# Depthwise taps in four column groups on TensorE, and products over 768 tokens in two halves of 384 columns

## What is computed

```python
def conv_module(h, w_pw1, w_dw, b_dw, ln_g, ln_b, w_pw2):
    u = h @ w_pw1
    a, gate = jnp.split(u, 2, axis=-1)
    u = a * jax.nn.sigmoid(gate)
    u = lax.conv_general_dilated(
        u, w_dw[:, None, :].astype(u.dtype), window_strides=(1,),
        padding=[(CONV_PAD, CONV_PAD)], dimension_numbers=('NWC', 'WIO', 'NWC'),
        feature_group_count=D_MODEL) + b_dw
    u = jax.nn.silu(layer_norm(u, ln_g, ln_b))
    return u @ w_pw2
...
        mod_l = jnp.split(sc @ w_mod[i] + b_mod[i], 6, axis=-1)
        hl = modulate(rms_norm(xl, norm1_g[i]), mod_l[0], mod_l[1])
        hc = modulate(rms_norm(xc, norm1_g[i]), mod_c[0], mod_c[1])
        if m == 0:
            ol = conv_module(hl, *cargs)
            oc = conv_module(hc, *cargs) if with_ctx else None
```

## Time and profile before

| what | value |
|---|---|
| median of 3 runs (range) | 2349.9 us (2349.07 to 2354.52) |
| the profiled execution | 2348.4 us |
| its span, mean granted clock of PE | 2346.1 us, 0.974 |
| PE, weight load, DVE, ACT, POOL busy | 95%, 76%, 60%, 34%, 28% of the span |
| products at L609 in the chain that ended last | 48% of the span |
| taps in that chain | 2% (PE, L2470) and 1% (DVE, L1748) |

### The profile page before, as it was taken

How to read it: one execution, slowest core, us unless ns; L and a number is a source line. 1 busy time by engine, 2 the same in 40 slices (tenths; PEclk the granted TensorE clock), 3 DMA queues, 4 the chain that set the end, 5 groups by cost and what they waited for, 6 DMA issues and landing times.

```text
span 2346.1 us, 30707 instructions
## 1 busy us (share of the span) xinstructions
PE 2223.6 (95%) x11666; PEld 1787.7 (76%) x11666; DVE 1417.1 (60%) x1872; ACT 807.3 (34%) x1145; POOL 667.5 (28%) x377
## 2 busy tenths in 40 slices
PE   6999969899999999998999999999997999899997
PEld 5677748788888888885457888887886888788885
DVE  5789982654444445544563754655418552699997
ACT  3212134211111111333663311111322543677775
POOL 0000014233333333431444344444542234011001
PEclk8999979999999999999999999999999999899999
DMA  9455532432222222220002233333232234599996
GB/s 309 156 160 169 198 124 81 179 138 63 63 63 63 63 63 63 66 72 10 10 1 64 83 98 92 97 98 113 72 90 63 63 76 153 188 394 403 406 405 252
DMA packets 248208, 312.12 MB, mean 133 GB/s; under 512 B 13642, under 2 KB 199595, under 8 KB 235827
## 3 DMA queue, kind: packets, MB, share of 16 engines
q1 hardware_dynamic: 236764, 275.33, 34.8%
q0 software_dynamic: 6688, 25.69, 2.8%
q10 hardware_dynamic: 4663, 9.79, 1.1%
HBM read 286.13 MB, written 24.65 MB: 132 GB/s over the span
## 4 chain that ended last, share of the span: by engine, by line
PE 84%; DVE 10%; ACT 2%; POOL 1%; DMA 1%; issue 1%; DVEq 0%; POOLq 0%; SPq 0%; ACTq 0%
PE acc L609 48%; PE acc L3013 8%; PE pb L3031 4%; PE acc L2524 3%; PE acc L2735 2%; PE pa L2749 2%; PE pb L2470 2%; PE pb L2762 2%; PE acc L661 2%; PE acc L643 2%; PE acc L2588 1%; DVE csum L1748 1%; DVE hid_hi L1813 1%; PE acc L690 1%; PE pa L2410 1%
## 5 line engine op out<-in xcount | busy, mean ns | idle before, releaser
L548 POOL TENSOR_TENSOR wlo<-raw,whi 128x1024 fp32r<-128x1024 f32 x180 | 449.5, 2498 | 907.1 <-ACT whi L537 887.0
L537 ACT ACTIVATE whi<-raw 128x1024 fp32r<-128x1024 f32 x188 | 198.4, 1059 | 890.3 <-PE acc L609 836.1
L609 PE MATMUL acc<-ah,whi 128*128 128x256 f32 (+1 forms) x1256 | 393.7, 362 | 5.0 <-DVE sg L2008 2.6
L609 PE MATMUL acc<-al,whi 128*128 128x256 f32 (+1 forms) x1256 | 389.4, 359 | 0.0
L609 PE MATMUL acc<-ah,wlo 128*128 128x256 f32 (+1 forms) x1256 | 388.9, 358 | 0.0
L609 PEld LDWEIGHTS acc<-ah,whi 128*128 128x128 f32 x1256 | 235.6, 189 | 48.3 <-issue 8.9
L609 PEld LDWEIGHTS acc<-ah,wlo 128*128 128x128 f32 x1256 | 236.7, 188 | 36.8
L609 PEld LDWEIGHTS acc<-al,whi 128*128 128x128 f32 x1256 | 236.7, 188 | 36.1 <-issue 0.5
L1833 DVE SCALAR_TENSOR_TENSOR x<-acc,mod,x 128x512 f32<-128x512 f32 (+1 forms) x174 | 109.7, 658 | 232.2 <-PE acc L609 232.1
L1037 DVE TENSOR_TENSOR expert_lo<-expert_pair,expert_hi 128x1024 fp32r<-128x1024 f32 x192 | 224.5, 1219 | 14.5 <-ACT expert_hi L1032 14.5
L1032 ACT ACTIVATE expert_hi<-expert_pair 128x1024 fp32r<-128x1024 f32 x192 | 201.4, 1059 | 63.4 <-PE acc L3013 40.1
(11 more groups left out here) (501 smaller groups left out, 3684.4 us busy)
## 6 DMA issues: line engine op xcount, KB each, us to landing
raw<-in_w_ff SPq DMA_DIRECT2D x128, 512.0 KB, 4.0
mod_raw<-in_w_mod SPq DMA_DIRECT2D x80, 512.0 KB, 5.8
expert_pair<-in_expert_w_gate SPq DMA_DIRECT2D x32, 1024.0 KB, 8.0
expert_pair<-in_expert_w_up SPq DMA_DIRECT2D x32, 1024.0 KB, 7.7
expert_pair<-in_expert_w_down SPq DMA_DIRECT2D x32, 1024.0 KB, 7.3
raw<-in_w_in SPq DMA_DIRECT2D x30, 512.0 KB, 3.8
raw<-in_conv_w_pw SPq DMA_DIRECT2D x24, 512.0 KB, 8.8
expert_rows_dram<-zero_rows POOLq DMA_DIRECT2D x1, 12288.0 KB, 38.1
```

Source lines behind the costliest of these rows:

```text
L537: e.eng.activation(whi[e.n["q"] % 2][:, :], raw[r][:, :], ACT.Copy).then_inc(S["hi_ready"], 1)
L548: e.eng.tensor_tensor(wlo[b][:, :], raw[e.n["g"] % RING][:, :], whi[b][:, :].bitcast(F32), ALU.subtract).then_inc(S["lo_ready"], 1)
L609: ins = e.eng.matmul(o, w, m, start=keys.index(key) == n, stop=len(keys) - 1 - keys[::-1].index(key) == n)
```

## The change

**Products.** `HALVES` takes the place of `FULL` wherever a product runs over 768 tokens: two matmuls of 384 columns in place of 256 and 512. The output then lies in columns 128 to 896 of the bank, so that each half is in a PSUM bank of its own; those who read it look there (`unit_at`, `all_cols`).

**Taps.** `TAP_BLOCKS` blocks of four taps in place of single taps on PE: 12 taps of tiles 0 to 5, 16 of tile 6 and 24 of tile 7. For each group `g` of 32 channels, `shifted[32 s + c, g, :]` holds `upb` of channel 32 g + c shifted by s, for the four shifts s; one matmul of 128 rows by 32 columns then adds four taps of 32 channels, and four of them, one for each group, write four different column groups of PE's array. So a block of four taps costs eight matmuls, and reads `shifted` with an offset of four per block. ACT issues 16 DMAs per tile that fill `shifted` (`shift_rows_of`, between `take_taps(i + 1)` and the copy of the second chunk), each 32 rows of 791 to 803 f32, about 101 KB. The matrices `tap_rows` are made by POOL, one tensor_tensor of 128 x 128 per block (`place_taps`), from 14 further columns of constants; the identity matrices scaled by ACT go. There is one buffer `shifted`: its fill waits for PE's taps of the tile before. PE does the taps of tile i - 1 where those of tile i stood; DVE takes the sum in an addition of its own (L1787) after tap 14.

**Others.** Both `split_low` of a tile go from DVE to POOL. `gated` stands after tap 10. Six more DMAs of constants.

```diff
-PE_TAPS = (0, 6, 6, 6, 6, 6, 6, 9)
+TAP_BLOCKS = (3, 3, 3, 3, 3, 3, 4, 6)
+GATE_AT = (16, 10, 10, 10, 10, 10, 10)
+SUMS_AT = (18, 15, 15, 15, 15, 15, 13, 6)
...
+    HALVES = [(0, TOK // 2, 1), (TOK // 2, TOK, 0)]
...
-        def make_diagonals(i):
-
-            act.wait_ge(S["taps_ready"], i + 1)
-            if i >= 2:
-                act.wait_ge(S["conv_summed"], i - 1)
-            for j in range(PE_TAPS[i]):
-                t = TAPS - PE_TAPS[i] + j
-                ins = act.activation(diag[:, j, :], mats[:, M_ID, :], ACT.Copy, scale=taps[i % 2][:, t:t + 1])
-            ins.then_inc(S["diag_ready"], 1)
+        def shift_rows_of(i):
+
+            act.wait_ge(S["glu_done"], i + 1)
+            if i:
+                act.wait_ge(S["conv_summed"], i)
+            width = wide + SHIFTS * (TAP_BLOCKS[i] - 1)
+            for g in range(4):
+                for s in range(SHIFTS):
+                    at = by_vector(i) + s
+                    act.dma_start(shifted[32 * s:32 * s + 32, g, 0:width], upb[i % 2][32 * g:32 * g + 32, at:at + width]
+                                  ).then_inc(S["shifted_in"], 16)
...
                 copy_row(chunks[0], pa[:, 0:512])
                 take_taps(i + 1)
-                make_diagonals(i + 1)
+                shift_rows_of(i)
                 if i:
                     copy_row(chunks[1], pa[:, 0:512])
...
+        def place_taps(i):
+
+            if i >= 2:
+                pool.wait_ge(S["conv_summed"], i - 1)
+            for j in range(TAP_BLOCKS[i]):
+                ins = pool.tensor_tensor(tap_rows[i % 2][:, j, :].rearrange("p (g c) -> p g c", g=4),
+                                         mod_pick[:, :].unsqueeze(1).to_broadcast([P, 4, 32]),
+                                         stacked_taps(by_vector(i) + SHIFTS * j, i).unsqueeze(2).to_broadcast([P, 4, 32]),
+                                         ALU.mult)
+            ins.then_inc(S["diag_ready"], 1)
...
+        for i in range(1, KT - 1):
+            split_first(e, split_low)
+            split_first(e, split_low)
+            if i < KT - 1:
+                place_taps(i + 1)
+            add_tile(i - 1)
...
-            if i < KT - 2:
-                for t in (20, 22):
-                    beside[t] = lambda: split_first(e, split_low)
...
-            for t in range(2, by_vector):
-                if t == late:
+            for t in range(2, by_vector(i)):
+                if t == SUMS_AT[i]:
                     dve.wait_ge(S["dve_chain"], e.at("c"))
-                    dve.wait_ge(S["conv_summed"], i)
+                    dve.wait_ge(S["conv_summed"], i + 1)
                     TT(csum[0][:, :], csum[0][:, :], pbk[:, 0:wide], ALU.add).then_inc(S["conv_taken"], 1)
...
         def conv_taps(i):
 
-            pe.wait_ge(S["glu_done"], i + 1)
-            pe.wait_ge(S["diag_ready"], i)
-            if i >= 2:
-                pe.wait_ge(S["conv_taken"], i - 1)
-            count = PE_TAPS[i]
-            for j in range(count):
-                t = TAPS - count + j
-                for c0, c1 in ((0, 512), (512, wide)):
-                    ins = pe.matmul(pbk[:, c0:c1], diag[:, j, :], upb[i % 2][:, t + c0:t + c1], start=j == 0,
-                                    stop=j == count - 1)
+            pe.wait_ge(S["shifted_in"], 256 * (i + 1))
+            pe.wait_ge(S["diag_ready"], i + 1)
+            if i:
+                pe.wait_ge(S["conv_taken"], i)
+            count = TAP_BLOCKS[i]
+            for c0, c1 in ((0, 512), (512, wide)):
+                for j in range(count):
+                    for g in range(4):
+                        part = slice(32 * g, 32 * g + 32)
+                        ins = pe.matmul(pbk[part, c0:c1], tap_rows[i % 2][:, j, part],
+                                        shifted[:, g, SHIFTS * j + c0:SHIFTS * j + c1], start=j == 0, stop=j == count - 1)
             ins.then_inc(S["conv_summed"], 1)
 
-        pair(FULL, 0)
+        pair(HALVES, 0)
...
             mod_chunk(first, pa[:, 0:512], after_product=i > 1)
-            conv_taps(i)
+            conv_taps(i - 1)
...
-        conv_taps(KT - 1)
+        conv_taps(KT - 2)
...
             mod_chunk(n, acc[1][:, 512 * (n % 2):512 * (n % 2) + 512], after_product=n == LAST_CHUNKS[0])
+        conv_taps(KT - 1)
```

More of the change, by code:

```diff
@@ L242, in _build @@
     taps = [sb(f"taps{b}", [P, 32], at=h_at + 12800 + 128 * b) for b in range(2)]
-    diag = sb("diag", [P, max(PE_TAPS), P], at=h_at + 16384)
+    tap_rows = [sb(f"tap_rows{b}", [P, max(TAP_BLOCKS[b::2]), P], at=h_at + 16384 + 2048 * b) for b in range(2)]
+    shifted = sb("shifted", [P, 4, PAD + CTX + PAD + LAT + 6], at=e_at)
     zero_rows = sb("zero_rows", [P, D], at=u_at)
@@ L493, in tap_sources, with by_vector, stacked_taps @@
         return ((taps[i % 2][:, 0:TAP_SPLIT], cols[:, C_TAP_A:C_TAP_A + 8 * TAP_SPLIT], column(i)),
-                (taps[i % 2][:, TAP_SPLIT:TAPS], cols[:, C_TAP_B:C_TAP_B + 8 * (TAPS - TAP_SPLIT)], column(i)))
+                (taps[i % 2][:, TAP_SPLIT:TAP_SPLIT + SHIFTS], cols[:, C_MORE_TAPS:C_MORE_TAPS + 8 * SHIFTS], column(i)))
+    def by_vector(i):
+        return TAPS - SHIFTS * TAP_BLOCKS[i]
+    def stacked_taps(first, i):
+        at = {11: C_VEC + 88 + 4 * i, 7: C_VEC + 120}.get(first, 384 + 8 * (first - TAP_SPLIT) + 4 * i)
+        return cols[:, at:at + 4]
     def chunk_at(n):
@@ L614, in run_group, with product @@
             ins.then_inc(S[last], 1)
-    def product(e, act_hi, act_lo, segs, k=KT, shift=0, out0=CTX, first="split_started", weights=None):
+    def product(e, act_hi, act_lo, segs, k=KT, shift=0, out0=None, first="split_started", weights=None):
         h, l = weights or (whi[e.n["q"] % 2], wlo[e.n["q"] % 2])
@@ L1191, in _, with rows_of_taps @@
             row += 8 * count
-        dw = A["conv_w_dw"][0].rearrange("t (c p) -> (t c) p", p=P)
         act.dma_start(vec_rows[0:120, 2, :], dw[0:120, :]).then_inc(S["consts_in"], 16)
-        act.dma_start(vec_rows[0:128, 3, :], dw[120:248, :]).then_inc(S["consts_in"], 16)
+        def rows_of_taps(row, n, first, tiles):
+            count = 4 * len(tiles)
+            act.dma_start(vec_rows[row:row + count, n, :].rearrange("m (s c) -> m s c", s=SHIFTS),
+                          A["conv_w_dw"][0][first:first + SHIFTS, P * tiles[0]:P * tiles[-1] + P].rearrange(
+                              "s (m c) -> m s c", c=32)).then_inc(S["consts_in"], 16)
+        for b in range(4):
+            rows_of_taps(32 * b, 3, TAP_SPLIT + SHIFTS * b, range(KT))
+        rows_of_taps(88, 1, 11, range(KT))
+        rows_of_taps(120, 1, 7, (KT - 1,))
         act.wait_ge(S["cols_ready"], 1)
@@ L1669, in _ @@
         dve.wait_ge(S["vec_turned"], 1)
-        for n, rows in enumerate((96, 88, 120, 128)):
+        for n, rows in enumerate((128, 124, 120, 128)):
             ins = dve.tensor_copy(cols[:, P * n:P * n + rows], pbk[:, P * n:P * n + rows])
@@ L1750, in conv_tile @@
                 e.n["c"] += 1
-                if t in beside:
-                    beside[t]()
+                if i < KT - 1 and t == GATE_AT[i]:
+                    gated(i + 1)
+                    tile_modulation(i)
             dve.wait_ge(S["dve_chain"], e.at("c"))
@@ L2443, in project @@
         def project(i):
-            product(e, ah, al, FULL, first="split_started" if i % 2 else None)
+            product(e, ah, al, HALVES, first="split_started" if i % 2 else None)
             e.n["g"] += 1
@@ L2619, in split_head @@
             e.n["q"] += count
-        pair(FULL, 1)
+        pair(HALVES, 1)
         mod_chunk(23, pa[:, 0:512])
         for i in range(2, KT - SPLIT_SLOTS):
-            product(e, ah, al, FULL)
+            product(e, ah, al, HALVES)
             e.n["g"] += 1
```

83 lines of the change are left out of this document (42 added, 41 removed).

## The result

| | before | changed |
|---|---|---|
| median (range) | 2352.21 us (2349.07 to 2355.79) | 2390.85 us (2390.18 to 2396.48) |
| ratio, 95% interval | | 1.0169 (1.0146 to 1.0192) |
| profiled execution, span, granted clock | 2348.4, 2346.1, 0.974 | 2396.48, 2394.5, 0.962 |

The change makes the kernel slower by 38.6 us, where 21 were forecast.

The account below looks back on a forecast made before the run. PE, busy 95% of the span, was taken as the bound. Five tiles +28.2, tile 1 -1.6, tail -5.4, start +0.3 and halves 0 gave +21.5 on 2348.4; stated 2371 us, range 2333 to 2395.

Parts of the forecast that it names:

- An issue at 0.42: Each of ACT's 16 shift DMA issues ahead of the second chunk's copy takes 0.42 us, 6.7 a tile.
- The clock at 1.8: In each long tile, PE's lower granted clock after its 7.1 us stop loses 1.8 us, bounds 0 and twice that.
- The tail at -5.4: From the last sigmoid to the last `cv`, 39.25 us before, the span shrinks to 33.9: -5.4.
- tile 1 at -1.6: In tile 1 PE's taps shrink, but chunk 7's product waits for its data: -1.6 us.
- The start: Six more constant DMAs end some 2.5 us later, mostly hidden by the wait for the input: +0.3 us.
- Rival 1: ACT's issues are cheap: at 0.05 us each a tile lasts 28.7, total 2333; chance 0.18 together with rival 2.
- rival 3: Both partly: an issue at 0.28 to 0.33 and no clock loss, +1 to +5 us, within the noise; chance 0.10.
- Rival 2: No lock between POOL and DVE's taps: a tile lasts 29.1, total 2335 us; chance 0.18 together with rival 1.
- Rival 4: Products in halves save half of their fixed part: -26 us on the sum, 2345; chance 0.03.
- Rivals 5 and 6: Column groups run one after another, 2440 us, chance 0.03; POOL becomes the bound, `wlo` late, 2395, chance 0.04.

Follow-up runs that it names:

- the half-issues kernel: The changed kernel with 8 shift DMAs in place of 16 for tiles 1 to 5: 2367.66 us.
- the swap: The changed kernel with the copy of the second chunk ahead of the 16 shift DMAs on ACT: 2336.07 us, ratio 0.9941 to the kernel before.
- the new order: Changed kernel, shift DMAs ahead of tap copies, second chunk between the products, next weights loaded earlier: 2322.8 us (splits on DVE), 2321.9 (on POOL).

## Why the prediction was wrong

**The mechanism held, link by link.** The copy of the second chunk is what ends PE's wait, behind `cv` and 16 issues; PE's blocks cost 4.1; the column groups run side by side; the order of the losses is the one foretold. The step that failed is the sizing of the terms, the price of an issue first: the trace shows 48.4 where the sum gave 21.5. Three terms were mis-sized:

- *An issue at 0.42.* It is 0.645 in the row of sixteen (0.612 and a pause), just over the upper bound of 0.63. I went by the rows that were nearest in their number of partitions. None of them had its source in SBUF, and that is what decides (442 ns from device memory, 612 within SBUF). The copies of the taps and the sixteen issues together take 10.3 (146.13 to 156.44) in place of 7.2, +3.1 a tile, 15.5 in all.
- *The clock at 1.8.* Turn and second product take 12.5 on the mean of the five tiles where 9.2 is full speed: 3.3 a tile, near the bound of 3.6, and 7.3 more in all than forecast. The row that I took was read to its end: behind the gap of 7.12 us the clock was back 3.9 us later, and a window from 459 to 470 us has 1.00. The slow stretches of the changed kernel last 5.0 to 7.9 us instead. Why they are longer is not shown; the length of the gap doesn't decide it, since gaps of 2.1 to 3.4 us in the half-issues kernel still lose 2.5 on the mean.
- *The tail at -5.4.* It came to +3.6. I added up all loads behind one another at 412 GB/s, to T + 22.7, and had the blocks follow. But I left the late chunk's landing at 13.3. SP asks for the last chunk at 334.8 (T + 6.3, where it was T + 15.2), while that late chunk is still on its way, and shifts and loads share the engines: the late chunk itself lands only at T + 22.5. The two chunk products and the turn that wait for it were in no term: 9.0 us at the lower clock, 4.5 at full speed.

Smaller: *tile 1 at -1.6* came to -0.2. Its second chunk's last piece was issued 0.5 later, took 9.05 in place of 8.6, and its last quarter cost 1.05 in place of 0.5; the shifts of that tile begin only at 108.97 and can't be the reason, which stays open. The start came to +0.4, as forecast (+0.3).

Against that `cv` came 1.1 a tile earlier than forecast: three taps took 5.83 beside the splits, 2.9 more than alone, where I had 4.1 (the first split begins 0.5 ahead of the first tap), and `tap_rows` cost 1.2 (0.94 of waiting, and 1.18 for a tap) in place of 1.4.

By terms, the five tiles came to 44.9 (forecast 28.2): +15.5 for issues and copies of the taps, +7.3 for the clock, -5.7 for `cv`, and about -1 for the halves' shorter products. The forecast lay some 17 us under the 38.6 of the medians and 27 under the trace, whose execution was the slowest.

**The rivals.** Rival 1, cheap issues: decided against, 0.645; and rival 3 with it, which needed 0.28 to 0.33 and no loss of clock. With rival 1 falls the use of the Trainium skill, page "DMA: Bandwidth & Descriptors", section "Issuing engines are not separate DMA queues", for this place: the issue time is small beside one transfer (landing after 2.2 to 3.4 us), but sixteen in a row are 10.3 us in front of whatever stands behind them. Rival 2, no lock: decided against (8.02 for four taps, 4.1 without POOL's splits). Rival 4, the halves: the sign was right and the size, 3.5 in place of 26, was not. Rivals 5 and 6 did not happen: a block costs 1.4, and POOL's splits take 2.7 each and no product of the stage's tiles waited for one.

## What to carry over

Price a row of DMA issues as work of the engine that issues them, at the duration of the same form, and look at what stands behind them in that engine's list: here one copy of 0.6 us, moved ahead of sixteen issues, turned 39 us lost into 12 gained. A change that takes work from the bounding engine pays only after the next link is moved too (load, copy, order of the chunks): of PE's 4 us a tile the change as it stood lost nine, the swap gained two, and the new order gained 4.4. And where a stop of PE is forecast, add what the clock takes behind it, from more than one such stretch: here they cost 1.9 to 4.0 us a tile, in no order of the stops' length.

## What was not expected of the hardware

An issue on ACT's queue costs 612 ns when the source is in SBUF and 442 when it is device memory, nearly the same from 8 KB to 101 KB and for 32 or 128 rows. PE's granted clock over the 5 us behind a stop is 0.50 after 8.7 us and after 2.7, 0.68 after 3.4 and 0.73 after 2.1, and it can fall after PE has begun again. And a pair of matmuls of 256 and 512 columns costs 6 ns more than two of 384 in every second tile of the convolution stage, and nothing more in the other tiles or in the MLP.
